# A three-block transformer kernel on one core: the first mixer's attention in pairs of heads, with projection and output units between its steps

## What is computed

```python
def mixer_ab(h, w_in, w_out, cmp_wk, cmp_wv, cmp_pe, sinks, rel_table):
    proj = h @ w_in
    qa, kca, vca, ksa, vsa, kwa, vwa, ga, qb, kb, vb = jnp.split(proj, ...)
    o_a = nsa_attention(qa, kca, vca, ksa, vsa, kwa, vwa, gates, cmp_wk, cmp_wv, cmp_pe, tab_a)
    o_b = swa_sink_attention(qb, kb, vb, sinks, tab_b)
    return jnp.concatenate([o_a, o_b], axis=-1) @ w_out
```

## Time and profile before

| | |
|---|---|
| median of 3 runs | 1153.72 us (1152.43 to 1157.09) |
| the profiled execution | 1155.67 us |
| its span | 1153.9 us |
| busy: PE / PEld / DVE / ACT / POOL | 92% / 88% / 68% / 43% / 1% |
| mean granted clock of PE | 0.953 |
| HBM read | 227 MB |
| first mixer, first projection to last output unit | 48 to 231 us |

### The profile page before, as it was taken

How to read it: one execution, slowest core, us unless ns; L and a number is a source line. 1 busy time by engine, 2 the same in 40 slices (tenths; PEclk the granted TensorE clock), 3 DMA queues, 4 the chain that set the end, 5 groups by cost and what they waited for, 6 DMA issues and landing times.

```text
span 1153.9 us, 20676 instructions
## 1 busy us (share of the span) xinstructions
PE 1060.1 (92%) x8107; PEld 1011.4 (88%) x8107; DVE 787.5 (68%) x1163; ACT 500.2 (43%) x845; POOL 9.1 (1%) x8
## 2 busy tenths in 40 slices
PE   1698799989999998999989999998999799999996
PEld 0598687989999997998979999998886799999995
DVE  4852678766677665777776676665688687677675
ACT  1431234354444444545435444434643346555552
POOL 1000000000000000000000000000000000000000
PEclk9898899999999998997989999999996699999998
DMA  9979543517777752890336777764554255555531
GB/s 374 302 263 172 196 145 110 191 56 269 277 260 282 276 182 83 306 338 5 128 128 213 289 270 280 267 216 150 211 191 158 73 217 179 186 175 190 180 128 37
DMA packets 58410, 229.44 MB, mean 199 GB/s; under 512 B 6384, under 2 KB 8432, under 8 KB 57840
## 3 DMA queue, kind: packets, MB, share of 16 engines
q1 hardware_dynamic: 58352, 228.64, 56.9%
HBM read 227.04 MB, written 1.57 MB: 198 GB/s over the span
## 4 chain that ended last, share of the span: by engine, by line
PE 79%; DVE 9%; DMA 6%; ACT 3%; issue 2%; SPq 1%; DVEq 0%; ACTq 0%
PE bank L1496 21%; PE bank L1497 21%; PE bank L1498 21%; DMA modbuf<-in_mod_w 5%; PE bank L1512 2%; PE bank L1582 2%; DVE acc L480 2%; DMA raw<-in_weights 1%; PE bank L1730 1%; PE bank L1612 1%; PE bank L1699 1%; PE bank L1520 1%; DVE x L1013 1%; PE bank L1698 1%; DVE otok L986 1%
## 5 line engine op out<-in xcount | busy, mean ns | idle before, releaser
L1496 PE MATMUL bank<-hH,wH 128*128 128x256 f32 x1632 | 470.9, 289 | 10.5 <-DVE hL L980 10.0
L1497 PE MATMUL bank<-hL,wH 128*128 128x256 f32 x1632 | 465.6, 285 | 0.0
L1498 PE MATMUL bank<-hH,wL 128*128 128x256 f32 x1632 | 465.4, 285 | 0.0
L933 DVE TENSOR_TENSOR wL<-raw,wH 128x1024 fp32r<-128x1024 f32 x273 | 324.4, 1221 | 141.3 <-ACT wH L646 141.0
L1496 PEld LDWEIGHTS bank<-hH,wH 128*128 128x128 f32 x1632 | 317.3, 194 | 16.4 <-issue 11.0
L646 ACT ACTIVATE wH<-raw 128x1024 fp32r<-128x1024 f32 x273 | 273.5, 1049 | 101.3 <-PE bank L1498 83.4
L1497 PEld LDWEIGHTS bank<-hL,wH 128*128 128x128 f32 x1632 | 317.2, 194 | 0.2
L1498 PEld LDWEIGHTS bank<-hH,wL 128*128 128x128 f32 x1632 | 317.1, 194 | 0.0
L1496 PE MATMUL bank<-aH,wH 128*128 128x256 f32 x528 | 150.2, 285 | 2.1 <-DVE aL L1131 2.1
L1497 PE MATMUL bank<-aL,wH 128*128 128x256 f32 x528 | 150.1, 284 | 0.0
L1498 PE MATMUL bank<-aH,wL 128*128 128x256 f32 x528 | 150.0, 284 | 0.0
(11 more groups left out here) (233 smaller groups left out, 1101.0 us busy)
## 6 DMA issues: line engine op xcount, KB each, us to landing
raw<-in_weights SPq DMA_DIRECT2D x273, 512.0 KB, 4.7
modbuf<-in_mod_w SPq DMA_DIRECT2D x48, 768.0 KB, 5.2
modbuf<-in_w_ada SPq DMA_DIRECT2D x32, 768.0 KB, 5.3
modbuf<-in_mod_w SPq DMA_DIRECT2D x14, 512.0 KB, 9.7
strips<-in_cmp_w SPq DMA_DIRECT2D x4, 512.0 KB, 11.0
strips<-bias_table SPq DMA_DIRECT2D x8, 256.0 KB, 10.8
otok<-in_mod_w SPq DMA_DIRECT2D x3, 512.0 KB, 15.5
acc<-in_mod_w SPq DMA_DIRECT2D x2, 512.0 KB, 11.2
```

The lines of the kernel that those rows point to most:

```text
L933: V.tensor_tensor(wL[:, slot, :], raw[:, slot, :], wH[:, slot, :].bitcast(F32), ALU.subtract).then_inc(lo_ready[c], 1)
L1496: mm(out, lhs_h, rhs_h, start=start, stop=False, skip_group_check=True)
L1497: mm(out, lhs_h, rhs_l, start=False, stop=False, skip_group_check=True)
L1498: return mm(out, lhs_l, rhs_h, start=False, stop=stop, skip_group_check=True)
```

## The change

- Heads go in pairs, head t on rows 0 to 63 and head t+4 on rows 64 to 127 of the tiles. There are 12 pairs: selected and windowed alternate for t = 0 to 3 (steps 0 to 7), then the sink heads (steps 8 to 11). `b` counts heads, two a step.
- The probabilities are divided by their sums and multiplied by the gate on DVE (`ab_weigh`) before they are transposed. Outputs are then feature-major, 128 features of a pair, and selected, windowed and compressed parts add up in one PSUM bank. `otok` and its transposes go; the outputs are split by ACT and DVE into `aH`, `aL`, `hH`, `hL` (`ab_features_high`, `ab_features_low`: one 128x256 piece of PSUM each).
- ACT, not DVE, copies the transposed probabilities (`ab_take_pt`).
- The output units are row blocks of `w_out` (one k tile, all 1024 outputs; `ab_out`), used as soon as a k tile is ready.
- Units 3 to 5 are the values, computed token-major with `h` stationary (`ab_values`); compression uses two 64-row halves, with `cw` in `otok`; compressed scores use a zero-padded `kc`.
- Projection units 8 to 15 stand in steps 0 to 7, output units 16 to 23 in steps 9 to 13 (`AB_FILL`); the dummy matmuls of the first mixer go. SP's list is written anew.

```diff
+        AB_PROJ = [0, 1, 2, 6, 7, 8, 9, 10, 11, 12, 13, 14, 15]
+        AB_TILE = [0, 1, 2, 3, 5, 6, 7, 8, 4, 9, 10, 11, 12]
+        AB_NUMBER = {e: n for n, e in enumerate(AB_PROJ)}
+        AB_STEPS = 14
+        AB_FILL = [[8], [9], [10], [11], [12], [13], [14], [15], [], [16], [17], [18], [19, 20], [21, 22, 23]]
...
+        AB_FT_STEP = [5, 6, 7, 9, 10, 11, 12, 13]
...
-            for p in range(2):
+            for p in range(RING):
                 load_unit(p)
-            sp.wait_ge(cw_zero, 1)
+            sp.wait_ge(table_out, 16)
+            for a in range(P // COPIES):
+                diag = bass.AP(A["table"].tensor, P - 1 - COPIES * a, [[16 * 512 - 1, COPIES], [512, 16], [1, S]])
+                sp.dma_start(strips[COPIES * a:COPIES * (a + 1), :, :], diag).then_inc(strips_landed, 16)
+            load_job(16)
+            load_job(17)
+            sp.wait_ge(h_ready, 4)
             for g in range(G):
-                sp.dma_start(cw[g * HD:(g + 1) * HD, g], A["cmp_w"][0]).then_inc(cw_landed, 16)
-            for p in range(2, RING):
+                sp.dma_start(cw[g * HD:(g + 1) * HD], A["cmp_w"][0]).then_inc(cw_landed, 16)
+            for p in range(6, 9):
                 load_unit(p)
...
+            load_job(18)
+            load_job(19)
+            sp.wait_ge(misc_psum, misc["cmpk"] + 1)
+            for g in range(G):
+                sp.dma_start(cw[g * HD:(g + 1) * HD], A["cmp_w"][1]).then_inc(cw_landed, 16)
+            load_job(20)
+            load_job(21)
+            for p in range(9, 12):
+                load_unit(p)
+            load_job(22)
+            load_job(23)
+            load_unit(12)
+            load_unit(13)
+            load_job(24)
+            for s in range(AB_STEPS):
+                for e in AB_FILL[s]:
+                    load_unit(e + RING)
+                load_job(25 + s)
+            load_job(39)
...
+            def ab_exp(b):
+                i = b % 2
+                act.wait_ge(neg_ready, b + 1)
+                if b >= 2:
+                    act.wait_ge(pt_psum, b - 1)
+                for q, (lo, up) in enumerate(((0, P), (P, 3 * P))):
+                    last = nc.scalar.activation(pr[:, i, lo:up], sn[:, i, lo:up], ACT.Exp, bias=nm[:, b, q:q + 1],
+                                                scale=-1.0, accum_out=sm[:, b, q:q + 1])
+                last.then_inc(prob_ready, 1)
...
+            def ab_take_pt(b):
+                act.wait_ge(pt_psum, b + 1)
+                if b >= 2:
+                    act.wait_ge(pv_done, b - 1)
+                nc.scalar.activation(pt[:, b % 2, 0:384], ab_turn_bank(b)[:, 0:384], ACT.Copy).then_inc(pt_ready, 1)
...
+            for s in range(AB_STEPS + 1):
+                for f in range(8):
+                    if AB_FT_STEP[f] == s - 1:
+                        ab_features_high(f)
+                if s < 12:
+                    ab_exp(2 * s)
+                    if s == 5:
+                        act.wait_ge(pcT_psum, 1)
+                        nc.scalar.activation(pcT, bank[3][:, 0:S], ACT.Copy).then_inc(pcT_ready, 1)
+                    if s >= 9:
+                        ab_take_pt(2 * s - 2)
+                    ab_exp(2 * s + 1)
+                if s == 3:
                     act.wait_ge(cmp_sub, 1)
...
+                    nc.scalar.activation(cp, cs, ACT.Exp, scale=-1.0).then_inc(cmp_exp, 1)
+                for e in AB_FILL[s] if s < AB_STEPS else ():
+                    if e < 16:
+                        ab_project(e)
+                if 1 <= s <= 12:
+                    if s < 9 or s == 12:
+                        ab_take_pt(2 * s - 2)
+                    ab_take_pt(2 * s - 1)
+                for e in AB_FILL[s] if s < AB_STEPS else ():
+                    if e >= 16:
+                        split_upto(min(e + 5, 27))
...
+            def ab_neg(b):
+                i, h = b % 2, ab_head(b)
+                strip, first = (h, 3e38) if b < 16 else (8 + h, nsink[:, h:h + 1])
+                dve.wait_ge(scores_psum, b + 1)
+                if b >= 2:
+                    dve.wait_ge(prob_ready, b - 1)
...
+            def ab_weigh(b):
+                i, h = b % 2, ab_head(b)
+                if b < 16:
+                    dve.wait_ge(prob_ready, b + 1)
+                else:
+                    dve.wait_ge(sink_exp, b - 15)
+                    link(V.tensor_tensor(sm[:, b, :], sm[:, b, :], sinkx[:, h, :], ALU.add))
+                link(V.reciprocal(sm[:, b, :], sm[:, b, :]))
+                for q, (lo, up) in enumerate(((0, P), (P, 3 * P))):
...
+                last.then_inc(weighed, 1)
...
+            split_upto(6)
+            compressed_input(0, 0)
+            split_upto(8)
+            compressed_input(1, 1)
+            jobs_upto(18)
+            take("cmpk")
+            dve.wait_ge(kc_zero, 1)
...
+            split_upto(9)
+            jobs_upto(21)
+            take("cmpv")
...
+            split_upto(11)
+            take("vrep")
+            for g in range(G):
...
+            split_upto(12)
+            jobs_upto(24)
+            take("gates")
+            taken(V.tensor_copy(gates_f, bank[7][0:24, 0:S]))
+            dve.wait_ge(misc_taken, misc["gatesT"] + 1)
+            link(V.tensor_scalar(small[:, 0:48], small[:, 0:48], 1.0, None, ALU.add))
+            link(V.reciprocal(gt[:, :, :].rearrange("p q n -> p (q n)"), small[:, 0:48]))
+            dve.wait_ge(strips_landed, 16 * (P // COPIES))
...
+            for s in range(AB_STEPS + 1):
+                for f in range(8):
+                    if AB_FT_STEP[f] == s - 1:
+                        ab_features_low(f)
+                if s < 12:
+                    ab_neg(2 * s)
+                    ab_neg(2 * s + 1)
+                if s == 1:
                     mod_vector(0, "mod0g", 16, 24)
...
+                if 1 <= s <= 12:
+                    ab_weigh(2 * s - 2)
+                    ab_weigh(2 * s - 1)
...
+                for e in AB_FILL[s] if s < AB_STEPS else ():
+                    split_upto(min(e + 5, 27))
+                jobs_upto(min(25 + s, JOBS_END[1]))
+            jobs_upto(JOBS_END[1])
...
-                    last = mm(bank[7][0:NCMP, 0:P], win[:, l, 0:NCMP], cw[:, :, l, :], start=(l == 0),
-                              stop=(l == CLEN - 1))
+                    for g in range(G):
+                        r = slice(g * HD, (g + 1) * HD)
+                        w, x_ = cw[r, l, :], win[r, l, 0:NCMP]
+                        if n == 0:
+                            last = mm(bank[7 - g][r, 0:NCMP], w, x_, start=(l == 0), stop=(l == CLEN - 1),
+                                      skip_group_check=True)
+                        else:
+                            last = mm(bank[7 - g][0:NCMP, 0:HD], x_, w, start=(l == 0), stop=(l == CLEN - 1),
+                                      skip_group_check=True)
...
+            def ab_values():
...
+                for q in range(QT):
+                    out = bank[q][:, 0:384].rearrange("p (c n) -> p c n", c=3)
+                    for k in range(KT):
+                        cols = slice(k * P, (k + 1) * P)
+                        h, l = hH[:, k, q * P:(q + 1) * P], hL[:, k, q * P:(q + 1) * P]
+                        mm(out, h, wH[:, 3:6, cols], start=(k == 0), stop=False, skip_group_check=True)
+                        mm(out, l, wH[:, 3:6, cols], start=False, stop=False, skip_group_check=True)
...
+                rows = [slice(i * HD, (i + 1) * HD) for i in range(2)]
+                for i in range(2):
+                    mm(ab_score_bank(2 * s + i)[:, 0:P], proj[rows[i], qt, 0:P], proj[rows[i], kt, 0:P], start=True,
+                       stop=True, skip_group_check=True)
+                for i in range(2):
+                    mm(ab_score_bank(2 * s + i)[:, P:3 * P], proj[rows[i], qt, P:2 * P], proj[rows[i], kt, :], start=True,
+                       stop=True, skip_group_check=True).then_inc(scores_psum, 1)
...
+            def ab_turn(b):
+                pe.wait_ge(weighed, b + 1)
+                if b >= 2:
+                    pe.wait_ge(pt_ready, b - 1 if b < 16 else b)
+                if b == 16:
+                    pe.wait_ge(fT_ready, 3)
+                for n in range(3):
+                    last = nc.tensor.transpose(ab_turn_bank(b)[:, n * P:(n + 1) * P], pr[:, b % 2, n * P:(n + 1) * P], ident)
+                last.then_inc(pt_psum, 1)
...
+                cols = [slice(i * HD, (i + 1) * HD) for i in range(2)]
+                for i in range(2):
+                    mm(o[cols[i], 0:S], vt[:, 0, vcol, cols[i]], pt[:, i, 0:S], start=first, stop=False,
+                       skip_group_check=True)
+                for i in range(2):
+                    last = mm(o[cols[i], P:S], vt[:, 1, vcol, cols[i]], pt[:, i, S:3 * P], start=False, stop=(s >= 8),
+                              skip_group_check=True)
+                    last.then_inc(pv_done, 1)
...
+            def ab_out(e):
+                kt = e - 16
```

(52 more changed lines are left out.)

453 lines of the change are left out of this document (189 added, 264 removed).

## The result

The changed kernel takes **1177.05 us** (median of four runs, 1173.68 to 1181.06), the kernel before 1153.08 (four runs, 1146.49 to 1157.09). The ratio is 1.0215, with a 95% interval of 1.0156 to 1.0274: slower by 24 us. The profiled execution takes 1175.44, its span is 1173.3 and the mean granted clock 0.932.

The account below looks back on a forecast made before the run. PE's own queue was taken to set the first mixer's 183 us. Afterwards 105 + 71 + 5 + 41.5 + 20 = 242.5, plus 15.5 for the clock, 258: 27 later, +1 behind, so 1182 us on the median's scale; range 1152 to 1196.

Parts of the forecast that it names:

- The start: First mixer before the attention steps: PE waits 10 us for the compression weights; scores are taken up at 105 us.
- Loop of steps 0 to 7: Attention steps 0 to 7: DVE, PE and ACT wait in turn, nothing overlapped, 8.6 us a step, together 71 at full clock.
- Step 8: Attention step 8, which has no dense unit: 5.1 us.
- Steps 9 to 11: Attention steps with PE's output unit inside the loop: 14.0 us each, 13.5 in step 9, 41.5 at full clock.
- The clock: First mixer: PE's idle gaps bring half clock, adding 4 us in steps 0 to 7, 9 in 9 to 11, 2.5 after; 15.5.
- The last steps: Steps 12 and 13, to the last output unit: 20 us at full clock, 2.5 more for the clock.
- PE's work: PE's work in the first mixer stage after the change: 112 us at full clock where 183 pass now.
- Behind the stage: After the first mixer: the norm waits for job 39, whose load waits for job 37, +1 us; cd and sb add nothing.
- (a): Rival for the first mixer: the clock stays up, same loops, 242.5 + 1 against 230.9, so 1167 us; chance 0.20.
- (b): Rival: strips yield to the compression weights and weigh is at its lower bound; stage 229, so 1153 us; chance 0.13.
- (c): Rival: hi splits run ahead of the exponentials, PE stays the queue, 1093 us; chance 0.13, partly for smaller gains.
- (d): Rival: half clock throughout the first mixer, PE needs 10.5 us a step and binds, 1196 us; chance 0.04.

## Why the prediction was right

The forecast, a stage made of a serial circle and a lost start, came true, and the sum of the stage was right within 2 us (259.5 for 258), in part by luck, as its errors cancelled:

| part of the forecast | predicted | profile after |
|---|---|---|
| start, to the first neg | 105 | 106.4 |
| steps 0 to 7 | 75 | 74.2 |
| step 8 | 5.1 | 7.0 |
| steps 9 to 11 | 50.5 | 46.2 |
| steps 12 and 13, to the last unit | 22.5 | 25.7 |
| sum | 258 | 259.5 |

- **The start** was right in size and cause: PE idle 11.2 us before the first compression, ended by the weights at 71.0, and the gates' job the last to come. What the prediction didn't say, and three runs showed, is that moving the strips alone doesn't give it back, and that more edits gave back half of it at most.
- **Loop of steps 0 to 7.** With the clock at 0.99 it measured 71.6, of which 1.3 were the dummies' own in step 1; predicted 71. Its terms: weigh 0.78 to 0.86 a head for 0.70 (bounds 0.5 and 1.0), the wait before the lo split 3.3 for 2.5. The run with early splits took away the one link that the loop hung on, and 21.6 us with it.
- **Step 8** was short by 1.9 us: I had left out that the negs of step 9 wait for scores that stand on PE behind step 8's turns and outputs (DVE idle 2.3 us there), so that PE's clock counts in this step. At full clock it was 5.3.
- **Steps 9 to 11.** At full clock the three steps come to 40.5, predicted 41.5. The wait before the lo split was 8 to 9.5 and not 6; my own terms for DVE (0.43, 1.52, 0.93, 1.22, 1.75) leave 8 of 14, so that number was a slip of subtraction.
- **The clock** was priced too high: 15.5 us predicted, about 12 by the estimate above. Steps 0 to 7 were right (3.8 for 4); the excess is in steps 9 to 11, 5.7 for 9. The granted clock was near the expected 0.75 (0.79 and 0.72), but I had counted 3 us a step as if the unit ran at half clock throughout; in the changed kernel the end of each unit (the last 4 to 14 of its 24 matmuls in steps 9 to 11) already ran at full.
- **The last steps** took 3.2 us more than 22.5. The walk had one unit left behind the last feature subtraction. PE had three behind the one before it, since `ab_pv(11)`, which waits for that subtraction, stands ahead of units 21 to 23 in its list:

```profile
248.48 0.65 PE L1903 MATMUL bank<-pt,vt 128*64 128x256 f32 x4 [3.21 <-DVE hL L1310]
```

From 249.3 the three units took 10.2 us, 8.6 at full clock. No run moved them.

- **PE's work**: 112 us at full clock was the sum; busy time in the stage was 152, above the 112 to 130 that the profile was to show. A mean clock between 0.74 and 0.84 accounts for most of that; the rest wasn't taken apart. It decided nothing.
- **Behind the stage** nothing was predicted but 1 us for job 39, which didn't show: the norm began with the last unit. The 7.4 us of the second mixer were in the base of the sum, the profiled execution of before, which I took at 2 us above its median. By the two profiles the stage costs 28.8 us and the kernel 19.4; by the medians the kernel costs 24. What follows the stage, the same instructions in every kernel here, took 913.8 to 918.8 us in the eleven profiles without the long stretch at half clock, 923.2 in the profile before and 913.8, the least of all, in the one after. So the distance between 24 and 28.8 is of the size of what executions differ by, and that the time came within 5 us of 1182 is partly luck.

**The rivals.** (a), the clock stays up, is out by the windows; with the clock up by eight dummies the time was 1172.44 and not its 1167, as the start, the last steps and the dummies keep their price. (b), no lost start and a cheap weigh: neither held. (c) named the condition by which the change would pay, the hi splits ahead of the exponentials. The kernel didn't have it; given it, the time fell by 23 to 33 us, with the reordered steps by 47, to 1130 and not to its 1093: a step of 0 to 7 was then 6.7 us, with PE busy for 6.3 of it (5.0 predicted) and DVE for 5.7, and the start stays. (d), half clock throughout, is out.

On the drain between tiling modes, weighed in the prediction by a page of the Trainium skill (TensorEngine Tiling (Array Packing), Key Properties), there are rows at full clock in the run with scores ahead of the unit:

```profile
182.29 0.49 PE L1881 MATMUL bank<-proj 64*128 64x128 f32 x4
182.62 0.60 PE L1884 MATMUL bank<-proj 64*128 64x256 f32 x4
183.15 0.38 PE L1585 MATMUL bank<-aH,wH 128*128 128x256 f32 x1
```

A pair's scores hold PE from 182.29 to 183.15, 0.86 us, where their columns are 0.64. The two heads do overlap (in series they would be 1.28), and 0.2 us are lost about the change of shape, where the bound gave 0.1 a change. The trace agrees with a drain of that size and doesn't show what the 0.2 us are made of. They are paid on PE, which decides nothing in steps 0 to 7.

## What to carry to other kernels

Shortening the bounding engine's list can be worth nothing, as here, if the new order of the others' lists makes a circle: before changing it, write down one step as a walk from engine to engine, and for each instruction on the walk ask whether it needs anything made in this step. Whatever doesn't (here the rounding of the next weights, the output unit, the next scores) goes ahead of what does; a few such moves turned a loss of 2% into a gain of 1.8% with the same instructions. Each cured wait uncovers the next one, so read the idle column again after every move.

## What the runs showed of the hardware

- For one list of instructions the granted clock of a stretch is a matter of the execution: a stretch of the second mixer ran at half clock for 13 to 14 us in three profiles of fourteen and for about 4 us or less in the others, 6 to 7 us apart. A single profile is not a base to half a per cent.
- An fp32 dummy of 128 columns is two records and 0.23 us; keeping the clock up was only free where the pause was longer than the dummies: twenty (4.6 us) cost nothing in pauses of about 7 us and delayed the turn by 3 us in a pause of 2.4; eight (about 2 us) cost 1.3 us in a step without a pause.
- Eight strip loads of 256 KB held the queue from 43 to 60 us at 89 to 177 GB/s with its share at 0.9 or more, and the loads issued behind them landed 17 to 20 us after their issue, where a unit's median over the execution is 4.7: moving such loads later moved the delay to whoever stood behind them.
